# Two modulation vectors move from TensorE's side work to VectorE, over half rows, in the first experts' stage

## The reference, cut to what matters

```python
c_lat = silu(c)[:, None, :]
c_con = silu(c_ctx)[None, None, :]
for i in range(2):
    mod_l = split(c_lat @ ada_w[i] + ada_b[i], 6)      # ada_w[i]: 1024 x 6144
    mod_c = split(c_con @ ada_w[i] + ada_b[i], 6)
    h = modulate(rmsnorm(x, norm_mix_g[i]), mod_l[0], mod_l[1])
    ...                                                # mixer 0: mLSTM, mixer 1: retention
    x = x + mod_l[2] * mixer_out
    h = modulate(rmsnorm(x, norm_ffn_g[i]), mod_l[3], mod_l[4])
    x = x + mod_l[5] * experts(h)                      # 16 experts, three 1024 x 1024 weights each
    ...                                                # the context tokens likewise in block 0
```

## Time and profile before

| | |
|---|---|
| median of 3 runs | 2554.59 us (2550.34 to 2562.33) |
| the profiled execution's own time | 2560.84 us |
| its span, first to last instruction | 2559.1 us |
| granted TensorE clock, mean of the span | 0.983 |
| TensorE busy | 2428.8 us, 95% |
| VectorE busy | 1201.3 us, 47% |
| ScalarE busy | 423.6 us, 17% |
| GpSimd busy | 304.5 us, 12% |
| bytes moved, mean rate | 597.11 MB, 233 GB/s |
| first experts' stage, TensorE's first expert product to the last | 489 to 1003 us |

### The profile page before, as it was taken

How to read it: one execution, slowest core, us unless ns; L and a number is a source line. 1 busy time by engine, 2 the same in 40 slices (tenths; PEclk the granted TensorE clock), 3 DMA queues, 4 the chain that set the end, 5 groups by cost and what they waited for, 6 DMA issues and landing times. The chain is left out here.

```text
span 2559.1 us, 53520 instructions
## 1 busy us (share of the span) xinstructions
PE 2428.8 (95%) x23863; PEld 1767.1 (69%) x23863; DVE 1201.3 (47%) x2185; ACT 423.6 (17%) x963; POOL 304.5 (12%) x262
## 2 busy tenths in 40 slices
PE   7999999899999998999999999888899989999999
PEld 4587665677777664588887654444467758888888
DVE  5785655511111115777686333323265566445632
ACT  2132541300000001200243000000011342210000
POOL 0010001022222220000001000000040302340000
PEclk9999999899999999999999999999999979999999
DMA  8472325799999996454307999999942210222220
GB/s 322 151 246 89 128 83 197 304 369 405 407 407 407 406 408 263 169 188 118 114 18 293 388 422 421 422 423 421 421 166 93 85 55 28 83 89 93 107 91 33
DMA packets 79889, 597.11 MB, mean 233 GB/s; under 512 B 10564, under 2 KB 17668, under 8 KB 34556
## 3 DMA queue, kind: packets, MB, share of 16 engines
q1 hardware_dynamic: 62540, 552.00, 54.0%
q0 software_dynamic: 14384, 31.20, 4.5%
q10 hardware_dynamic: 2736, 10.49, 1.0%
HBM read 576.50 MB, written 17.41 MB: 232 GB/s over the span
## 5 line engine op out<-in xcount | busy, mean ns | idle before, releaser
L1787 PE MATMUL moe_ps<-room,moe_xs 128*32 128x256 f32 x9568 | 537.0, 383 | 46.2 <-DMA room<-in_experts 42.6
L1787 PEld LDWEIGHTS moe_ps<-room,moe_xs 128*32 128x32 f32 x9568 | 355.6, 111 | 226.9 <-issue 40.4
L1787 PE MATMUL moe_ps<-room,moe_hid_t 128*32 128x256 f32 x4432 | 248.5, 382 | 5.6 <-DMA room<-in_experts 5.3
L1787 PEld LDWEIGHTS moe_ps<-room,moe_hid_t 128*32 128x32 f32 x4432 | 160.5, 111 | 95.1 <-issue 15.0
L2061 DVE SCALAR_TENSOR_TENSOR x_feat<-moe_ps,mod,x_feat 128x512 f32<-128x512 f32 (+1 forms) x144 | 95.9, 730 | 135.3 <-PE moe_ps L1861 124.9
L777 PE MATMUL hout_ps<-h_feat,room 128*128 128x256 f32 x696 | 159.1, 380 | 0.0
L2128 DVE TENSOR_TENSOR moe_hid<-moe_hid,moe_ps 128x512 f32<-128x512 f32 x32 | 22.0, 688 | 279.0 <-PE moe_ps L1787 279.0
L777 PEld LDWEIGHTS hout_ps<-h_feat,room 128*128 128x128 f32 x696 | 132.3, 190 | 18.5 <-issue 0.5
L2148 DVE TENSOR_SCALAR moe_y<-moe_ps,moe_gates 128x256 f32<-128x256 f32 x42 | 17.7, 478 | 265.4 <-PE moe_ps L1787 265.4
L2004 ACT ACTIVATE moe_hid<-moe_ps 128x512 f32<-128x512 f32 x32 | 19.1, 597 | 741.6 <-PE moe_ps L1787 706.9
L1833 POOL DMA_INDIRECT acc<-moe_y,moe_sum_ids x42 | 69.6, 1657 | 292.6 <-DVE moe_y L2148 284.0
(11 more groups left out here) (695 smaller groups left out, 3777.5 us busy)
## 6 DMA issues: line engine op xcount, KB each, us to landing
room<-in_experts SPq DMA_DIRECT2D x140, 2048.0 KB, 30.5
room<-in_experts SPq DMA_DIRECT2D x67, 1024.0 KB, 22.5
moe_slot<-in_experts SPq DMA_DIRECT2D x30, 1024.0 KB, 41.3
room<-in_ffn_gate SPq DMA_DIRECT2D x9, 1024.0 KB, 4.8
room<-in_ffn_down SPq DMA_DIRECT2D x6, 1408.0 KB, 7.0
room<-in_ada_first SPq DMA_DIRECT2D x8, 1024.0 KB, 13.1
qk_ada_w<-in_ada_w SPq DMA_DIRECT2D x8, 1024.0 KB, 5.0
room<-in_ada_t POOLq DMA_DIRECT2D x16, 512.0 KB, 8.9
```

Source lines behind the costliest of these rows:

```text
L1787: mm = pe.matmul(group_ps(part, g)[32 * q:32 * q + 32], turned[:, k * GROUP:(k + 1) * GROUP], weights[:, m, q], start=(k == 0 and g != 1), ...
```

## The change

`qk` makes only (0, 2) beside its products and `mout` makes none. Eight pieces of 16 matmuls, two pairs of transposes and eight loads of 1 MB go. The part (0, 3) takes the place of (1, 0) among the two parts that `mlstm_values` makes by rows, so the number of tiles there stays. The retention layer keeps its four parts.

A new class `HalfRows` makes (0, 5) and (1, 0) in the first experts' stage, for both conditions. Its tiles are half as long, 128 x 512 (256 KB): 2 halves x 2 parts x 8 tiles = 32 tiles in 16 pairs. A first half's sum starts from the bias and is kept, the second half's sum starts from the first's. ScalarE issues the loads: a pair is loaded behind the silu of an expert's gate, after VectorE has used the pair before it; at pairs 0 and 8 two loads of 256 KB bring a half of the two conditions, and ScalarE applies silu to them. VectorE makes four row products for each pair, between an expert's transpose of the hidden rows and the scaling of its output. The product that nobody reads goes to a free PSUM bank.

```diff
-ROW_PARTS = [(1, n) for n in range(N_MOD)]
-ROWS_EARLY = 2
+SIDE_PARTS = [(0, 2), (0, 4)]
+ROW_PARTS = [(0, 3), (1, 1), (1, 2), (1, 3), (1, 4), (1, 5), (0, 5), (1, 0)]
+ROWS_EARLY, ROWS_KEYS = 2, 6
...
+class HalfRows:
...
+    def load_pair(self, act, pair):
+        sig = self.sig
+        m = 2 * pair
+        if m >= len(self.tiles):
+            return
+        if m:
+            act.wait_ge(sig["used"], m)
+        half = self.tiles[m][0]
+        columns = slice(half * self.HALF, (half + 1) * self.HALF)
+        begins = m % self.each == 0
+        if begins:
+            for r in range(2):
+                act.dma_start(self.cond[:, r], bass.AP(self.dram["cond_rows"].tensor, r * D + half * self.HALF,
+                                                       [[0, P], [1, self.HALF]])).then_inc(sig["cond"], 16)
+        for room in range(2):
+            _, layer, part, n = self.tiles[m + room]
+            act.dma_start(self.rooms[:, room], self.dram["ada_t"][ROW_PARTS.index((layer, part)) * KT + n][:, columns]
+                          ).then_inc(sig[f"landed_{room}"], 16)
+        if begins:
+            act.wait_ge(sig["cond"], 32 * (half + 1))
+            act.activation(self.cond[:], self.cond[:], ACT.Silu).then_inc(sig["silu"], 1)
+
+    def work_pair(self, dve, pair):
...
+            for r, product in enumerate((self.product, tile)):
+                so_far = self.sums[:, r, i:i + 1]
+                begin, to = (so_far, K.mod[:, layer, r, KT * part + n, :]) if half else (
+                    K.col("ada_b", 48 * layer + KT * part + n), so_far)
+                dve.tensor_tensor_reduce(product, tile, self.cond[:, r], 1.0, begin, ALU.mult, ALU.add, to
+                                         ).then_inc(sig["used" if r else "products"], 1)
...
@@ mlstm_attention: mout
-                     add_gated(K, 0, 0), make="begun", mods=[(0, 5)], pieces_at=(9, 13, 17, 21), turned_at=3, ps=ps,
+                     add_gated(K, 0, 0), make="begun", ps=ps,
...
@@ mlstm_projections: qk
-            seven(nc, K, dram, "qk", feed, K.h, halves, evacuate, mods=[(0, 2), (0, 3)], after=convolve_now,
+            seven(nc, K, dram, "qk", feed, K.h, halves, evacuate, mods=[(0, 2)], after=convolve_now,
...
@@ experts_stage, ScalarE
+                    if mods:
+                        mods.load_pair(act, 0)
                     gate(0)
+                    if mods:
+                        mods.load_pair(act, 1)
                     for e in range(LAST):
...
                         gate(e + 1)
+                        if mods:
+                            mods.load_pair(act, e + 2)
...
@@ experts_stage, VectorE
+                        if mods and e == 0:
+                            mods.work_pair(dve, 0)
                         dve.wait_ge(sig["w_used"], used_up(e, UP))
...
                         dve.transpose(hid_t[:].rearrange("p g c -> p (g c)"),
                                       hid[:].rearrange("p g c -> p (g c)")).then_inc(sig["hid_t"], 1)
 
+                        if mods and e < LAST:
+                            mods.work_pair(dve, e + 1)
```

## The result

The changed kernel takes 2565.75 us (median of 20 runs, 2559.48 to 2570.51); the kernel before 2558.73 us (20 runs, 2550.34 to 2563.71; they take in the three runs of the table ahead of the prediction). The ratio is 1.0028, 95% interval 1.0021 to 1.0035: a loss of 7.0 us, well inside what the forecast called no change, and of the sign it gave. The profiled execution is 2570.51 us, the longest of the 20 (span 2568.6 us).

What follows compares the result with a forecast made beforehand. The prediction took the first experts' stage to be bound by weights arriving through full DMA engines, TensorE elsewhere. Loads' 21.2 us less 9.9 won gave +11.3 on 2554.6, so 2565.9 us, range 2558 to 2577.

Steps and rivals of the forecast that it cites:

- no change: Whole kernel: a difference within about 0.5%, 12.8 us, which a measurement cannot tell from none; chance 0.53.
- The bound: First experts' stage: the last weights' arrival through full DMA engines sets its end; in keys' and output products TensorE binds.
- What goes: Keys' and output products: side pieces and transposes leave TensorE's stream, 4.97 us for each part, 9.9 us won.
- Rival 3: Keys' stage: VectorE's convolution becomes late, so that saving is lost; +16.2 us, 2570.8 us; chance 0.04.
- VectorE and ScalarE: First experts' stage: row products of 0.65 to 1.3 us and ScalarE's loads fit into waits; cost nothing.
- Rival 4: Experts' rounds: a tile comes late, VectorE scales an output late and TensorE waits; 8 us more, 2573.9; chance 0.04.
- The price of a load: First experts' stage, full DMA engines: 95 ns a 2 KB packet, 0.76 us a load, 21.2 us for 28.
- The free loads: First experts' stage: conditions' first half and pairs 0 to 2 find idle engines, leaving 28 of 36 loads to pay.
- Rival 1: The 28 loads: short packets cost more, 0.81 us each or above, a loss past 12.8 us; chance 0.35.
- Rival 2: First experts' stage: the tiles' loads ride free, only the 9.9 us gain is seen, 2544.7 us; chance 0.06.
- Rival 5: The 28 loads: each takes the engines for its whole 2.6 us; +62.9 us, 2617.5 us; chance 0.02.
- The signs: Changed profile: landing time grows faster, first chunk wait about 100 us earlier, waits total 21 us, VectorE's wait 13 to 16.

Runs made afterwards that it cites:

- `loads_only`: The changed kernel with all 36 loads, but VectorE's row products take 8 of 512 columns; ratio to the kernel before 1.0030, experts' stage 506.7 us.
- `work_only`: The changed kernel with all 64 row products, but 4 loads instead of 36; ratio to the kernel before 0.9955, experts' stage 488.7 us.
- `side_gone`: The changed kernel without the half rows, (0, 5) and (1, 0) a constant 0.5, side pieces gone too; ratio to the kernel before 0.9964.
- `outputs_bare`: The kernel before with (0, 5) left out, a constant 0.5, so no side work in the output products; ratio to the kernel before 0.9982.
- `loads_twice`: `loads_only` with each tile loaded twice and conditions' loads cut to 8 columns, 64 loads instead of 36; ratio to the kernel before 1.0101.

## Why the prediction was right

**The bound, right.** The stage is limited by bytes through full DMA engines while TensorE reads 100% busy. `loads_only` and `work_only` show it from both sides: 506.7 us with the loads alone, 488.7 with the work alone.

**What goes, right.** 9.9 us forecast; -9.2 (`side_gone`) and -11.5 us (`work_only`) by the runs, products 2.58 us apart, the experts' first product 10.7 us earlier after and 9.5 in `side_gone`. Half of it alone, in the output products, is -4.6 against 4.97 (`outputs_bare`). Rival 3 falls: no product of the keys' stage waits for VectorE.

**VectorE and ScalarE, right.** Nothing waits for them; 0.74 us a product lies between the bounds of 0.65 and 1.3. Rival 4 falls: the two tiles of expert 0 came late, by 7.3 us together, and the slack of the earlier trace rows covered them; no later one by more than 0.21 us.

**The price of a load, too high.** This is the term that was mis-sized. The prediction took 95 ns for a packet of 2 KB, from the step between 8 and 4 KB packets, which gives a fixed part of 311 - 2 x 144 = 23 ns. The queue shows 86 ns and a fixed part of some 10. That is 0.69 us a load instead of 0.76: 28 x 0.07 = 2.0 us. Half of the error lies in the reading of the two rows. The prediction let the packets of the earlier trace rows fill exactly 100% of the engines, while SyncE's queue had these shares in the two windows:

```profile
q1 hardware_dynamic: 577, 4.20, 101.1%
```

```profile
q1 hardware_dynamic: 432, 1.57, 99.2%
```

Read as the 86 ns were read, from the queue's own share, the packets take 315 and 165 ns, the halving saves 150, and the next one would save 75: 90 ns, 0.72 us a load. The nearest row was that of ScalarE's stores, 0.70, which the prediction listed and passed over; bytes alone, 0.647, missed by less than 0.76 too. The load of the same shape, 0.85, was read from engines that were not full, and lay furthest off of the near rows. Why it costs more there, no run settles.

**The free loads, one too few.** Eight were taken; the first 80 us show nine, the line through three kernels meets zero near 11. With nine the sum becomes 27 x 0.69 = 18.6 us, less 9.9: +8.7. The stage grew by 17.5 to 18.3 us. Two things lie between 18.6 and that: the shares of the full window add up to 102.7%, so that 0.69 us by share is 0.67 us of the stage's time (the slope from 36 to 64 loads is the same 0.67), and six kernels without the loads differ by 1.4 us in this stage. The runs have +7.0 us for the whole, where +11.3 was forecast; 2.0 and 0.7 us of the difference have these two causes, the other 1.6 lie within the interval of the ratio (1.8 us either way).

**Luck in the number.** The median came out at 2565.75 us for a forecast of 2565.9, but the forecast set its 11.3 us on a median of three runs, 2554.6, and the kernel before has 2558.7 in twenty. A base 4.1 us too low met a loss 4.3 us too high.

**The rivals.** Rival 1 (packets dearer than 0.81 us a load) is refuted by 0.69. Rival 2 (tiles ride free) would have given `side_gone`'s time. Rival 5, each load for its whole 2.6 us, would be 28 x 2.6 = 73 us more for the further loads of `loads_twice`, where the stage grew by 18.8. The Trainium skill (DMA: Bandwidth & Descriptors, Anatomy of one DMA — SWDGE (gpsimd) path) gives the fixed 2.0 us as a fit for loads that GpSimd issues, and says itself that they are mostly completion latency; the section Measured, which the prediction names, has the advice to batch. The trace agrees that it is latency: 0.69 us of engine time against 0.647 by bytes leaves 0.04 us.

**The signs.** The time to landing was to grow by 0.134 us per us from 550 us on, which put the first wait for a chunk near 750 us. It grew by 0.17, and the wait came at 738.89; between the two windows of the earlier trace rows, which the prediction used, it grew no more than before (19.8 against 20.5 us): TensorE began to wait in between, and from then on it stayed near 38 us. The waits for chunks were to add up to the 21 us: they sum to 21.7 us in the stage, but 8.4 of these were there before. Of the 18.3 us by which the stage grew, 13.3 stand as waits; 4.5 stand as busy time of TensorE, 483.9 us for the 8832 matmuls that took 479.4 before; why, no run settles. VectorE's wait of 13 to 16 us: 16.03. The wait ahead of the last up product: 4.25 us, still there.

## What to carry to other kernels

Read a busy engine together with the trend of the time to landing in the same stage. Here TensorE was 100% busy beside full DMA engines while the time to landing kept growing: it lived on a stock. What was added then counted by its bytes (36 loads, 17.5 us), and 64 row products on VectorE did not count. Before moving loads into such a stage, multiply their bytes by its rate (here 0.69 us for 256 KB) and compare with what the move frees; only what fits into idle transfer time at the stage's start is free. A half idle stage is not a free place either: look at what runs on GpSimd when VectorE gets the work, and at what else the issuing queue has to ask for.

## What the runs showed of the hardware

- Under full load the same 256 KB cost little more in packets of 1 KB (48 ns each, 0.76 us) than in packets of 2 KB (86 ns each, 0.69 us). The expected fixed part of a packet was 23 ns, the measured one is about 10.
- A row product on VectorE, which reads two operands from SBUF, took 2.81 and 2.83 us instead of 1.28 when GpSimd read and added 768 columns beside it; GpSimd's add took 2.66 us beside it (the rows above), and 1.81 in the kernel before. Where the row product had begun first (399.28, GpSimd's copy at 399.68), it kept its 1.28 us and the copy took 1.57 instead of 0.82. The Trainium skill (SBUF — State Buffer, Who interferes with whom) says that a VectorE instruction with two SBUF inputs contends with a GpSimd instruction that reads SBUF; these rows agree that the two slow each other.
